# First two expert rows fetched on a partial top-k, one set of keys sorted during the queries, the second head's queries moved behind row 0

## What is computed

```python
q = (xt @ w_q).reshape(t, PEER_HEADS, 2, PEER_HALF)                 # 8 heads, 2 halves of 128
sub_scores = jnp.einsum('thcd,hckd->thck', q, sub_keys)             # 2 sets of 128 keys per head
vals, ids = lax.top_k(sub_scores, PEER_TOPK)                        # best 16 of each set
cand = vals[:, :, 0, :, None] + vals[:, :, 1, None, :]              # 16 x 16 sums
top_sc, pos = lax.top_k(cand.reshape(t, PEER_HEADS, 256), PEER_TOPK)
i1 = jnp.take_along_axis(ids[:, :, 0], pos // PEER_TOPK, axis=-1)
i2 = jnp.take_along_axis(ids[:, :, 1], pos % PEER_TOPK, axis=-1)
eid = (i1 * PEER_N_KEYS + i2).reshape(t, PEER_HEADS * PEER_TOPK)    # 128 experts per token
gate = jax.nn.softmax(top_sc, axis=-1)
...
act = jax.nn.gelu(jnp.einsum('td,tkd->tk', xb, u_tab[eb]))
out = jnp.einsum('tk,tkd->td', gb * act, v_tab[eb])                 # then residual, final rms_norm
```

## Time and profile before

| | us |
|---|---|
| median of 3 runs | 3370.12 (3369.14 to 3372.43) |
| the profiled execution's own time | 3369.07 |
| its span, first to last instruction | 3367.2 |
| TensorE busy in the span | 3075.1 (91%) |
| VectorE busy | 1922.0 (57%) |
| ScalarE busy | 1278.0 (38%) |
| GpSimd busy | 366.2 (11%) |
| mean granted TensorE clock, share of full speed | 0.982 |

### The profile page before, as it was taken

How to read it: one execution, slowest core, us unless ns; L and a number is a source line. 1 busy time by engine, 2 the same in 40 slices (tenths; PEclk the granted TensorE clock), 3 DMA queues, 4 the chain that set the end, 5 groups by cost and what they waited for, 6 DMA issues and landing times.

```text
span 3367.2 us, 43494 instructions
## 1 busy us (share of the span) xinstructions
PE 3075.1 (91%) x18098; PEld 2404.7 (71%) x18098; DVE 1922.0 (57%) x2855; ACT 1278.0 (38%) x2353; POOL 366.2 (11%) x361
## 2 busy tenths in 40 slices
PE   8999999999999999999999999998987767777776
PEld 8888988999999999988989998444443323332332
DVE  6546565554555555676765544555555555555554
ACT  4535455443534445565544343222222222222222
POOL 1001000100000000100000001221232222122221
PEclk9989999999999999999999999999999989999999
DMA  7435445555555555544445446999999999999997
GB/s 216 155 119 177 161 164 194 178 185 188 178 185 184 180 188 192 203 150 163 151 165 211 138 169 274 430 431 430 431 420 431 431 427 432 430 431 430 431 430 338
DMA packets 94338, 911.08 MB, mean 271 GB/s; under 512 B 10360, under 2 KB 14840, under 8 KB 19132
## 3 DMA queue, kind: packets, MB, share of 16 engines
q0 software_dynamic: 37680, 540.03, 37.6%
q1 hardware_dynamic: 48816, 344.95, 29.5%
q10 hardware_dynamic: 7644, 23.30, 2.2%
HBM read 898.81 MB, written 9.44 MB: 270 GB/s over the span
## 4 chain that ended last, share of the span: by engine, by line
PE 67%; DMA 22%; DVE 6%; ACT 3%; issue 1%; ACTq 0%; POOL 0%; DVEq 0%; POOLq 0%
PE sums L552 15%; PE sums L553 15%; PE sums L554 15%; PE sums L1005 10%; DMA area<-in_uv,cst 9%; DMA hT<-in_uv,cst 5%; DMA ringx<-in_uv,cst 4%; DMA ring<-in_uv,cst 2%; PE sums L961 2%; PE sums L600 2%; PE sums L602 1%; PE sums L601 1%; DVE area L2203 1%; ACT cst L1050 1%; DVE wl L1662 1%
## 5 line engine op out<-in xcount | busy, mean ns | idle before, releaser
L1662 DVE TENSOR_TENSOR wl<-ring,wh 128x1024 fp32r<-128x1024 f32 x612 | 749.8, 1230 | 612.2 <-ACT wh L1050 611.3
L1050 ACT ACTIVATE wh<-ring 128x1024 fp32r<-128x1024 f32 x612 | 643.7, 1054 | 494.3 <-PE sums L554 439.3
L1050 ACT ACTIVATE cst<-cst 128x1 f32<-128x1 f32 (+2 forms) x786 | 234.1, 299 | 903.9 <-DVE cst L2203 843.6
L1005 PE MATMUL sums<-area,cst 128*128 128x512 f32 x984 | 459.5, 614 | 96.5 <-ACT cst L1050 96.4
L1005 PEld LDWEIGHTS sums<-area,cst 128*128 128x128 f32 x984 | 184.5, 194 | 353.3 <-issue 192.1
L2203 DVE CUSTOM_DVE_ANT_0 area<-area 128x2048 f32<-128x2048 f32 x123 | 281.7, 2291 | 256.7 <-DMA area<-in_uv,cst 256.7
L552 PE MATMUL sums<-normed,wh 128*128 128x256 f32 x1440 | 407.6, 283 | 0.0
L554 PE MATMUL sums<-normed,wl 128*128 128x256 f32 x1440 | 407.4, 283 | 0.0
L1005 PE MATMUL sums<-ringx,cst 128*128 128x512 f32 x656 | 302.6, 607 | 63.6 <-ACT cst L1050 63.6
L554 PE MATMUL sums<-hidden,wl 128*128 128x256 f32 x1024 | 290.2, 283 | 0.0
L553 PE MATMUL sums<-normed,wh 128*128 128x256 f32 x1024 | 290.2, 283 | 0.0
(11 more groups left out here) (332 smaller groups left out, 5763.4 us busy)
## 6 DMA issues: line engine op xcount, KB each, us to landing
ring<-in_w_in_a SPq DMA_DIRECT2D x66, 1024.0 KB, 4.9
ring<-in_w_up SPq DMA_DIRECT2D x64, 1024.0 KB, 4.9
ring<-in_w_down SPq DMA_DIRECT2D x64, 1024.0 KB, 4.8
ring<-in_w_out SPq DMA_DIRECT2D x32, 1024.0 KB, 4.9
ring<-in_w_in_b SPq DMA_DIRECT2D x16, 1024.0 KB, 4.8
ring<-in_w_xk SPq DMA_DIRECT2D x16, 1024.0 KB, 5.2
ring<-in_w_xv SPq DMA_DIRECT2D x16, 1024.0 KB, 4.9
ring<-in_w_xq SPq DMA_DIRECT2D x16, 1024.0 KB, 5.0
```

What stands on the lines that cost most here:

```text
L1005: mm = te.matmul(sums[t][:, 512 * i:512 * i + 512], diag[:, n % 2, :], v[:, 512 * i:512 * i + 512], start=False, stop=n % 128 == 127)
L1050: return sc.activation(out, in_, f, **kw)
L1662: ve.tensor_tensor(wl[:, j % 3, :], ring[:, load % 3, j % 2 * 1024:j % 2 * 1024 + 1024], wh[:, j % 3, :], ALU.subtract).then_inc(lo_in, 1)
```

## The change

Five edits, all at the start of the expert stage but the second.

1. `first_two`, new, inside `topk(0)`: after the best eight of each set are known, VectorE works out the expert numbers of rows 0 and 1 alone. Row 0 is the best key of each set; row 1 is the better of (best, second) and (second, best). `eid_in` counts three times for head 0: row 0, row 1, rows 2 to 15. GpSimd waits accordingly.
2. `steps_before`: 8 steps ahead of row 0 in place of 16, then 8 for each 7 rows up to row 13, 24 steps ahead of row 14, and then 5 for each 8 rows as before. All 64 are made ahead of row 78, where it was row 77.
3. TensorE makes the scores of set 0 in the middle of the second chunk of `first_queries`; ScalarE evicts each set by itself, and VectorE waits for each set by itself. The counts of `scr_in` and `sub_mm` move by one for it.
4. The pieces of `topk(1)` stand ahead of dots 8, 9, 10 and 11, no longer 0, 2, 4 and 6.
5. ScalarE's exponential for the first gate stands behind one query chunk, no longer two.

```diff
-        TOP_AT = (0, 2, 4, 6)
+        def top_at(g):
+            return (0, 2, 4, 6) if g else (8, 9, 10, 11)
         def steps_before(n):
-            return min(64, 16 + 5 * n // 8)
+            return 8 + 8 * n // 7 if n < 14 else min(64, 24 + 5 * (n - 14) // 8)
...
+                        elif k == 8:
+                            on.wait_ge(keys_in, 16)
+                            on.wait_ge(qp_in, 1)
+                            on.wait_ge(rd_mean, RD_MEANS["ffn"])
+                            sub_scores(0, (0,), (0,))
...
-                on.wait_ge(rd_in, FACTORS["ffn"] + 1)
-                on.wait_ge(sub_mm, 1)
-                act(scr[:, 0, 0:T], banks[6][:, 0:T], ACT.Copy, scale=rc[:, 0:1]).then_inc(scr_in, 1)
+                        on.wait_ge(rd_in, FACTORS["ffn"] + 1)
+                    on.wait_ge(sub_mm, n + 1)
+                    z = slice(n * P, (n + 1) * P)
+                    act(scr[:, 0, z], banks[6][:, z], ACT.Copy, scale=rc[:, 0:1]).then_inc(scr_in, 1)
...
-                    if done.n == 2:
+                    if done.n == 1:
                         gate_exp(0)
...
+            def first_two():
+                x = eq[:, 0, :]
+                own(ve.tensor_copy(idf[:, :, 0:2], ids[:, :, 0:2]))
+                on.wait_ge(v_seq, seq.n)
+                ve.scalar_tensor_tensor(eid[:, 0, 0:1], idf[:, 0, 0:1], 128.0, idf[:, 1, 0:1], ALU.mult,
+                                        ALU.add).then_inc(eid_in, 1)
+                for a in range(2):
+                    b = 1 - a
+                    own(ve.tensor_tensor(x[:, a:a + 1], vals[:, 0, a:a + 1], vals[:, 1, b:b + 1], ALU.add))
+                    own(ve.scalar_tensor_tensor(x[:, 2 + a:3 + a], idf[:, 0, a:a + 1], 128.0, idf[:, 1, b:b + 1],
+                                                ALU.mult, ALU.add))
+                on.wait_ge(v_seq, seq.n)
+                own(ve.tensor_tensor(x[:, 4:5], x[:, 0:1], x[:, 1:2], ALU.is_ge))
+                own(ve.tensor_tensor(x[:, 5:6], x[:, 2:3], x[:, 3:4], ALU.subtract))
+                on.wait_ge(v_seq, seq.n)
+                ve.scalar_tensor_tensor(eid[:, 0, 1:2], x[:, 5:6], x[:, 4:5], x[:, 3:4], ALU.mult,
+                                        ALU.add).then_inc(eid_in, 1)
...
+                    if g == 0 and c == 1:
+                        first_two()
...
-                on.wait_ge(eid_in, n // 16 + 1)
+                on.wait_ge(eid_in, n + 1 if n < 2 else n // 16 + 3)
```

More of the change, by code:

```diff
@@ L943, in first_queries @@
                         mm.then_inc(sums_mm, 1)
-                on.wait_ge(keys_in, 16)
                 on.wait_ge(qp_in, 2)
-                on.wait_ge(rd_mean, RD_MEANS["ffn"])
-                sub_scores(0, (0,))
+                sub_scores(0, (0,), (1,))
                 off(on, len(EVICTIONS) - 1)
@@ L968, in expert_queries @@
                         h = n // 2
-                        on.wait_ge(scr_in, h)
+                        on.wait_ge(scr_in, h + 1)
                         on.wait_ge(qp_in, n + 3)
@@ L982, in turn_rows, with sub_scores @@
                     mm.then_inc(tr_mm, 1)
-            def sub_scores(h, tiles):
+            def sub_scores(h, tiles, sets=(0, 1)):
                 for t in tiles:
-                    for c in range(2):
+                    for c in sets:
                         o = 256 * t + P * c
@@ L1040, in tensor @@
                     on.wait_ge(qp_in, 18)
-                    on.wait_ge(scr_in, 9)
+                    on.wait_ge(scr_in, 10)
                     begin(1)
@@ L1488, in query_chunk @@
                 if n >= 4:
-                    on.wait_ge(sub_mm, n // 2)
+                    on.wait_ge(sub_mm, n // 2 + 1)
                 act(qp[:, n % 4, y], banks[4 + n % 2][:, y], ACT.Copy).then_inc(qp_in, 1)
@@ L1492, in query_chunk @@
                     h = n // 2
-                    on.wait_ge(sub_mm, h + 2)
+                    on.wait_ge(sub_mm, h + 3)
                     for t in ((0, 1) if h else (1,)):
@@ L1581, in scalar @@
                 weigh(n)
-                if n % 16 == TOP_AT[2] and n < 240:
+                if n % 16 == top_at(n // 16)[2] and n < 240:
                     gate_exp(n // 16 + 1)
@@ L2139, in memory @@
                 yield "+m3"
+            def first_two():
[15 more added lines that the diff above has]
+                                        ALU.add).then_inc(eid_in, 1)
             def topk(g):
                 t, h = g // 8, g % 8
-                on.wait_ge(scr_in, h + 2 if g else 1)
+                if g:
+                    on.wait_ge(scr_in, h + 3)
                 for c in range(2):
+                    if g == 0:
+                        on.wait_ge(scr_in, c + 1)
                     s = scr[:, h, 256 * t + P * c:256 * t + P * c + P]
@@ L2189, in topk @@
                     on.wait_ge(v_seq, seq.n)
-                ve.scalar_tensor_tensor(eid[:, t, 16 * h:16 * h + 16], sel[:, 0, :], 128.0, sel[:, 1, :], ALU.mult,
-                                        ALU.add).then_inc(eid_in, 1)
+                e0 = 0 if g else 2
+                ve.scalar_tensor_tensor(eid[:, t, 16 * h + e0:16 * h + 16], sel[:, 0, e0:16], 128.0,
+                                        sel[:, 1, e0:16], ALU.mult, ALU.add).then_inc(eid_in, 1)
                 on.wait_ge(top_a, g + 1)
@@ L2262, in vector @@
                     pieces = topk(n // 16 + 1)
-                if n % 16 in TOP_AT and n < 240:
+                if n % 16 in top_at(n // 16) and n < 240:
                     next(pieces)
```

## The result

The changed kernel takes 3374.59 us, the median of 21 runs (3367.19 to 3378.41); the kernel before, run beside it, takes 3369.18 us, also over 21 runs (3364.39 to 3372.60). The ratio is 1.0015, with a 95% interval of 1.0010 to 1.0021: 5.4 us slower, 3.4 to 7.1. That is smaller than the 0.2% which the prediction took as the least that counts, but its interval does not touch 1. The forecast was no change.

A forecast was written before the change was run, and what follows sets the result against it. The DMA, full at about 431 GB/s, bounds the kernel: its start, plus bytes, plus holes. 3369.07 - 6.5 (start) + 2.3 (rows 1 to 18) + 5.2 (row 80) = 3370.1 us, range 3364.5 to 3375.5.

The forecast's parts named there:

- The bound: Whole kernel: the end is when the DMA starts to be full, plus the bytes, plus the holes.
- The start: First gathers: row 0's issued at 2051.75, 8.9 us earlier, DMA full from 2053.4; -6.5 us (-6.1 to -7).
- Row 0's sum: Row 0's sum at about 2065, before 2083.20; row 5's gather at 2069, before 2088.87; nothing runs dry up to there.
- Row 80: First row in the ring, waiting for the last query step, now one row later: the hole widens by 5.2 us.
- Rows 1 to 18: TensorE becomes the slower one; short hole at row 19 and one clock drop: +2.3 us (0 to +6).
- The clock drops at each break: Slower rival, rows 1, 7, 11 and 14: four drops give 3375.5 us, a fifth 3377.3; chance 0.12 for five or more.
- The start is kept: Faster rival: neither hole opens, at row 19 or row 80, or the start gains more; 3362.6 us, chance 0.12.
- The change does not release row 0 early: Rival: new waits of ScalarE or TensorE stop set 1, start only 1 us earlier; 3373.3 us, chance 0.04.
- The sum: Whole kernel: 3369.07 - 6.5 + 2.3 + 5.2 = 3370.1 us, no change that the measurement tells; chance 0.76.

The follow-up runs named there:

- The early start taken back: Changed kernel without first_two, rows 0 to 15 released together: 3376.83 us; also with 5 steps per 8 rows from row 7 and FEW = 90: 3370.10 us.
- the old order: Changed kernel with steps_before and the places of the topk(1) pieces as before, rows 0 and 1 still released early: 3365.79 us to 3368.92 of the kernel before.
- The last steps earlier: Changed kernel with its 64 query steps ended ahead of row 72, not row 78: 3366.20 us to 3368.92 of the kernel before, ratio 0.9993.
- the ring's rows from 90: Changed kernel with the query weights' ring first used as row buffers at row 90, not 80: 3368.50 us to 3370.66 of the kernel before.
- the kernel with the old density: Changed kernel with 5 steps per 8 rows from row 7, ring from row 90, top-k pieces of heads 2 to 4 moved: 3363.45 us to 3370.66 before.

## Why the prediction was where it was

**The bound** stands: start, bytes, holes.

**The start** was forecast at -6.5 us (-6.1 to -7) and measured -6.1. Every step of it came within 0.2 us on before's clock: set 1's first eight at 2050.25 (2050.35), the first gather at 2051.62 (2051.75), the rest's at 2059.84 (2060.0). The early start taken back, with either order, gives 5.0 and 4.85 of it to the two rows' early release.

**Row 0's sum** and what it frees: 2065.11 (2065) and 2068.99 (2069). Nothing ran dry, as said; the old order shows what it would have been without this part, 4.7 us at row 5.

**Row 80**: the last step one row later, hole 6.6 us in place of 2.0, +4.6 to a forecast of +5.2. The last steps earlier and the ring's rows from 90 both close it, so place and size are shown.

**Rows 1 to 18** is the step that failed, by its size. The prediction had "just late: 0.3 to 0.5 us of hole" at row 19 and one clock drop, "+2.3 us (0 with no drop and a quicker start, up to +6 with three)"; it measured +6.1. The mechanism is right, TensorE the slower one until row 14, and the kernel with the old density, whose stage is 4.2 us shorter than its like's, shows it. Taken apart:
- The wait stands ahead of row 2, not of row 1. I had rows 0 and 1 share the DMA with chunk loads; they landed ahead of them, and row 1's dot starts at 2066.94 for 2070. Row 2 pays instead. Up to row 2's end this changed nothing: 2083.46, and by the forecast's prices 2083.4.
- I counted one clock drop ahead of row 14 and there are two, at rows 2 and 7. Row 14 ends at 2162.87 in place of 2160.6 (2158.8 and the drop). The kernel with the last steps earlier has the same order up to there and no drop at row 2 (TensorE, below). From the first load of `w_pq` its row 14 starts 1.57 us earlier, and its early loss is 5.0 us in place of 6.2 (6.5 with only the ring's rows from 90, which has both drops). So the second drop is worth 1.2 to 1.6 us by these profiles, one of each kernel, and with the single drop that I counted the term would still have been about 5.

```profile
2080.66 3.70 PE L1009 MATMUL sums<-area,cst 128*128 128x512 f32 x8 [2.50 <-ACT cst L1054]
```

- Row 19's gather started later than I let it. It goes out at 2166.75, and its bytes come 2.8 us later, not 1.6:

```profile
2168.00:2169.00 1.00, 1.00 (x4) 0.49 (x3) 0.93 (x7) 0.50 (x2) 0.87 (x1) 1.00 0.04 16
2169.00:2170.00 1.00, 1.00 (x5) 0.50 (x4) 0.93 (x5) 0.05 (x1) 0.00 (x0) 1.00 1.21 246
```

  GpSimd's issue of it takes 2.12 us, where row 0's took 1.02, and the first bytes follow the end of the issue by 0.7 us in both. That is 1.2 us of hole.
- Together: by the forecast's reckoning, with its one drop, row 19's bytes start at 2162.8 and the DMA is dry from 2161.1 on, 1.7 us (it wrote 0.3 to 0.5 for the hole without the drop, where 2158.8 + 0.6 + 1.6 is 2161.0 and leaves none; so its 2.3 should have been 1.7). The issue was 2.1 us later than that, at 2163.30 on before's clock, and the start 1.2, which makes 5.0. A row is 2.10 MB and not 2.11 (GpSimd's queue moves 536.89 MB from 2045 us on; the other 3.15 MB are moved before the stage), so the DMA was dry 0.6 us sooner. The last 0.5 us lie in a thin start behind the hole.
- The DMA is short of full before that: from 2120 to 2160 it moves 405 GB/s, 387 to 415 in stretches of 10 us, and loses 2.4 us. It dips where one gather ends and the next has only just started: 2130 to 2133, below, is where row 12's bytes end and row 13's, issued at 2127.18 with 2.07 us, begin. I reckoned with a DMA that is full or empty, and did not see this; but it is a part of the 6.1 and no further term. What is not moved there is moved later, and row 19's issue is set by TensorE: the sums of rows 7 and 14 start 46.4 us apart here and 46.3 in the kernel with the last steps earlier, which loses nothing from 2122 to 2142 (431 GB/s) and 4.0 in place of 3.5 us around row 19.

```profile
2130.00:2133.00 3.00, 3.00 (x11) 1.72 (x10) 2.83 (x8) 1.21 (x3) 0.66 (x1) 1.00 0.93 328
```

**The rivals.** *The clock drops at each break* comes nearest in its time (3375.5 for four), in part by luck: it counted four drops and there were two, and the late start of row 19 and the other items above made up the rest. *The start is kept* did not happen here, but it is what the kernel with the old density and the ring's rows from 90 comes close to: its holes are 1.1 us more than before's. *The change does not release row 0 early* is ruled out by 2051.62.

**The sum**, -6.1 + 6.1 + 4.6 = +4.6 (+1.0 was forecast), lies inside the ratio's 3.4 to 7.1; nothing is left over that the measurement can tell. The chance was too sure of "no change" because I gave the unknown size of a chain of 14 rows the value of its simplest case.

**The clock.** Waits of 1.84 us were followed by 3.70 at row 14 and by 5.40 at row 7 of the same trace; one of 2.81 by 3.70 at row 11 and one of 2.51 by 5.40 at row 2. The prediction read from the earlier trace rows that waits of 1.90 us and more are followed by a drop and that of 1.84 is not. The trace of the kernel before already had rows that say otherwise:

```profile
2262.74 3.70 PE L1005 MATMUL sums<-area,cst 128*128 128x512 f32 x8 [2.38 <-ACT cst L1050]
...
2354.37 5.16 PE L1005 MATMUL sums<-area,cst 128*128 128x512 f32 x8 [1.84 <-ACT cst L1050]
```

The Trainium skill, in "TensorE: Matmul & The Clock Gate", on HAM oscillation, has TensorE fall back each time that it waits on transfers. Of the changed kernel's four waits only row 2's goes back to a transfer (its dot waited 5.58 us for the row). Five kernels come to row 2 in the same order: waits of 2.51, 2.65 and 2.73 us were followed by 5.40, 5.12 and 5.40, and waits of 2.50 and 2.89 by 3.70. They agree in three cases of five, and the length of the wait doesn't part them. What does stays open. For a forecast it is a price of up to 1.8 us with a chance, at every such wait.

## What to carry to other kernels

When the bytes of one queue set the end, an earlier start is worth its bytes only if every later buffer is released in time: go through the releases behind it as closely as through the start, and give each its slack. Work that is moved off the path at the start has to go somewhere; here 8 steps for 7 rows ahead of row 14 gave back all 6.1 us, and the old 5 for 8 over more rows, with the first use of the last buffers put 10 rows later, kept 5 of them. And when two traces differ ahead of the first changed instruction, count both from an event behind that difference, or the difference of the profiles will be laid to the change.

## What the runs showed that I had not expected

- The DMA falls short before it is dry: 405 GB/s from 2120 to 2160. In this time the changed kernel has issued 0.5 to 1.7 rows more than its queue has moved; the kernel before, at 430 GB/s, 1.5 to 2.9. That this backlog is the cause is argued from these rows, not shown by a run of its own.
- The same code ahead of the stage took 2028.98 to 2038.34 us from profile to profile, with the granted clock between 200 and 260 us at 0.86 in one and 0.81 in the other. This is as large as the effect that was measured.
- GpSimd's issue of a gather takes 0.94 to 1.13 us in all 190 rows of the changed kernel where no dot of VectorE runs in its first 0.94 us. Of the 66 where one does, 42 take more than 1.2 us, up to 2.9. Where the queue has other gathers to move this costs nothing (row 79, 2.48 us); where it is idle the bytes wait, as at row 19 and at row 5 of the old order (2.36 us, first bytes at 2095.08).
